# Delta heads 2 and 3 pause for eight rounds behind their second step, and six more output pieces stand beside the last rounds

## What is computed

```python
o_a = sliding_window_attention(qa, ka, va, sinks)    # 8 query heads, window 128
o_b = gated_delta_rule(qb, kb, vb, g, beta)          # 4 heads of 128, chunks
o_b = o_b * rsqrt(mean(o_b * o_b) + eps) * norm_w * silu(z)
return concatenate([o_a, o_b], axis=-1) @ w_out      # 1024 x 1024
```

```python
v_new = u_c - w_c @ S
o_c = q_c @ S + qk_c @ v_new
S = S * exp(gl_c) + kt_c.T @ v_new
```

## Time and profile before

| what | value |
|---|---|
| median of 3 runs | 2363.33 us (2363.24 to 2363.87) |
| profiled execution | 2363.01 us |
| its span in the trace | 2360.9 us |
| PE busy | 2318.6 us, 98% |
| DVE, ACT, POOL busy | 1425.1, 1076.6, 262.5 us |
| mean granted TensorE clock | 0.998 |

### The profile page before, as it was taken

One profiled execution on the slowest core, in us unless ns is written; L12 is line 12 of the kernel. 1 busy time (PEld: TensorE's weight loads), 2 busy tenths in 40 slices (PEclk: granted clock), 3 DMA queues, 4 the chain that ended last, 5 costly groups with the idle time before them and its releaser, 6 DMA issues.

```text
span 2360.9 us, 32407 instructions
## 1 busy us (share of the span) xinstructions
PE 2318.6 (98%) x13256; PEld 1945.5 (82%) x13258; DVE 1425.1 (60%) x2184; ACT 1076.6 (46%) x1853; POOL 262.5 (11%) x235
## 2 busy tenths in 40 slices
PE   9998999999999999999999999999999999999997
PEld 7777888888888988888968888888887779888886
DVE  6786764434587753433775677636486446775455
ACT  5655363223278542322555654434254555444341
POOL 0041320000221400000420011100000001110000
PEclk9999999999999999999999999999999999999999
DMA  5220133233223233222221232232221112322222
GB/s 210 81 67 3 39 106 98 98 98 97 82 99 98 81 107 98 97 93 96 96 81 59 77 99 98 99 98 91 92 94 55 53 39 95 101 93 96 98 90 63
DMA packets 60643, 207.48 MB, mean 88 GB/s; under 512 B 7072, under 2 KB 9168, under 8 KB 60368
## 3 DMA queue, kind: packets, MB, share of 16 engines
q1 hardware_dynamic: 59856, 202.66, 26.3%
q0 software_dynamic: 640, 2.76, 0.3%
HBM read 201.93 MB, written 2.10 MB: 86 GB/s over the span
## 4 chain that ended last, share of the span: by engine, by line
PE 85%; DVE 9%; ACT 3%; issue 1%; POOL 0%; DMA 0%; SPq 0%; another core or an unknown queue 0%; DVEq 0%; ACTq 0%; POOLq 0%
PE ps L288 25%; PE ps L290 25%; PE ps L289 25%; DVE WL L261 1%; DVE TM L633 1%; DVE AR L858 1%; PE ps L2908 1%; PE ps L348 1%; PE ps L2937 1%; PE ps L2921 1%; PE ps L350 1%; PE ps L349 1%; PE ps L1841 1%; DVE X L636 1%; DVE XL L658 0%
## 5 line engine op out<-in xcount | busy, mean ns | idle before, releaser
L288 PE MATMUL ps<-XH,WH 128*128 128x512 f32 (+1 forms) x2120 | 794.7, 375 | 8.2 <-DVE WL L831 5.8
L290 PE MATMUL ps<-XH,WL 128*128 128x512 f32 (+1 forms) x2120 | 779.4, 368 | 0.0
L289 PE MATMUL ps<-XL,WH 128*128 128x512 f32 (+1 forms) x2120 | 779.1, 367 | 0.0
L261 DVE TENSOR_TENSOR WL<-RAW,WH 128x1024 fp32r<-128x1024 f32 (+1 forms) x378 | 462.6, 1228 | 176.8 <-ACT WH L249 176.0
L288 PEld LDWEIGHTS ps<-XH,WH 128*128 128x128 f32 x2120 | 400.6, 189 | 85.8 <-issue 8.6
L249 ACT ACTIVATE WH<-RAW 128x1024 fp32r<-128x1024 f32 (+1 forms) x378 | 386.8, 1035 | 153.5 <-DMA RAW<-in_w 124.2
L290 PEld LDWEIGHTS ps<-XH,WL 128*128 128x128 f32 x2120 | 400.4, 189 | 66.4
L289 PEld LDWEIGHTS ps<-XL,WH 128*128 128x128 f32 x2120 | 400.9, 189 | 65.4 <-issue 2.2
L288 PE MATMUL ps<-H,WH 128*128 128x512 f32 (+1 forms) x1200 | 431.0, 359 | 1.6 <-DVE AR L858 1.0
L289 PE MATMUL ps<-H,WH 128*128 128x512 f32 (+1 forms) x1200 | 429.5, 358 | 0.0
L290 PE MATMUL ps<-H,WL 128*128 128x512 f32 (+1 forms) x1200 | 429.5, 358 | 0.0
(11 more groups left out here) (426 smaller groups left out, 2337.3 us busy)
## 6 DMA issues: line engine op xcount, KB each, us to landing
RAW<-in_w SPq DMA_DIRECT2D x128, 512.0 KB, 3.4
RAW<-in_up SPq DMA_DIRECT2D x88, 512.0 KB, 3.4
RAW<-in_dn SPq DMA_DIRECT2D x32, 512.0 KB, 3.4
RAW<-in_hyb SPq DMA_DIRECT2D x20, 512.0 KB, 3.4
RAW<-in_qkv SPq DMA_DIRECT2D x18, 512.0 KB, 3.5
RAW<-in_kvf SPq DMA_DIRECT2D x17, 512.0 KB, 3.5
RAW<-in_rin SPq DMA_DIRECT2D x16, 512.0 KB, 3.4
RAW<-in_dn SPq DMA_DIRECT2D x16, 384.0 KB, 3.0
```

The costliest lines, as they stand in the source:

```text
L261: dve.e.tensor_tensor(WL[:, s, 0:n], RAW[:, s, 0:n], f32(WH[:, s, 0:n]), ALU.subtract).then_inc(*w_lo.at(u))
L288: pe.e.matmul(out, wh, xh, start=first, stop=False)
L289: pe.e.matmul(out, wh, xl, start=False, stop=False)
L290: return pe.e.matmul(out, wl, xh, start=False, stop=last)
```

## The change

`hybrid_rounds` leaves heads 2 and 3 out of rounds 3 to 10 (`rounds` counts the finished ones, so 2 to 9), on all four engines. When heads 0 and 1 are over, six more pieces are added to those that `ahead(2)` may use.

```diff
+        LATE = 8
+
         def hybrid_rounds(heads, att, ahead):
-            over, rounds, left = set(), 0, 12
+            over, rounds, left, more = set(), 0, 12, 6
             while len(over) < 5:
-                for g in heads[0:2] + [att] + heads[2:4]:
+                for g in heads[0:2] + [att] + (heads[2:4] if rounds < 2 or rounds >= 2 + LATE else []):
                     if g not in over and next(g, "end") == "end":
                         over.add(g)
                 rounds += 1
+                if heads[0] in over and heads[1] in over:
+                    left, more = left + more, 0
                 if att in over and left and rounds >= 28:
                     ahead(2)
                     left -= 2
-            ahead(left)
+            ahead(left + more)
```

## The result

The changed kernel takes 2376.97 us (median of 4 runs, 2373.03 to 2379.85) beside 2363.3 us before (2363.24 to 2363.87). The ratio on record is 1.0052, with a 95% interval of 1.004 to 1.0064: 12.3 us slower, 9.5 to 15.1 by the interval. The profiled execution took 2376.9 us. Two things are to be seen at once: the loss is twice the forecast, and the runs of the changed kernel lie 6.8 us apart, where those of the kernel before lay within 0.7 us.

The account below looks back on a forecast made before the run. TensorE bounds the kernel, carrying 85% of the chain. Terms: -4.0 won, +8.0 steps moved, -4.3 today's waits and handovers replaced, +1.4 at round 20 and w, +5.0 tail: +6.1, 2369.4 us; range 2365.8 to 2372.6.

Parts of the forecast that it names:

- The gain of rounds 3 to 10: Window rounds without heads 2 and 3: the window's loop of 3.4 us limits them, so round 20 begins 4.0 us earlier.
- No wait in this stage did that today: Clock rule: a 2.20 us wait elsewhere halved TensorE's clock, none in this stage; the new 2.5 us wait might.
- The steps of rounds 20 to 33: Heads 2 and 3 run eight steps late: 8.0 us of TensorE steps move behind the window; norms begin at 254.6.
- the walk: The prediction's round-by-round timing of the changed stage, from the window's maxima at 163.51 to the stage's end at 279.7.
- The wait at w: Round 23, w products: one wait of 1.15 us where three stand in a row today.
- The tail: From the norms' start to the stage's end: 25.1 us, with 2.5 us idle before the last six pieces.
- Rival (1): TensorE's clock falls behind the new wait before head 2's pieces: +7.7 us, 2371.0; chance 0.20.
- The six pieces themselves are moved, not added: nothing: The six pieces put beside the last rounds add no time of their own.
- Rival (2): A smaller loss: the woken heads' value blocks hide and w doesn't wait; +3.3 us, 2366.6; chance 0.20.
- (3): Not slower: the window's loop is no bound, rounds 3 to 10 fall to 2.8 us; -0.8 us, 2362.5; chance 0.08.
- (4): The six pieces find heads 0 and 1 unready and stand as waits: +8 us, 2371.3; chance 0.04.

Follow-up runs that it names:

- the repeat: Experiment 1: the changed kernel run again unaltered; 2374.51 us (2373.00 to 2378.75) beside 2364.06 before, ratio 1.0044.
- fill_all: Changed kernel with unread products of ones added in TensorE's waits of rounds 4, 5, 6, 8 and behind head 3's norm; 2374.15 us beside 2364.7.
- experiment 8: Changed kernel with heads in the order 0, 2, 1, 3 from round 21 on; 2375.67 us beside 2364.06 before, ratio 1.0048.
- experiment 6: Changed kernel without the six pieces beside the last rounds, 12 there and 12 behind; 2374.76 us beside 2365.2 before, ratio 1.0036.
- experiment 9: Changed kernel with heads 2 and 3 left out of two rounds instead of eight; 2372.62 us beside 2364.06 before, ratio 1.0032.

## Why the prediction was wrong, step by step

**The sign and the order of events were right, the size was half.** The likeliest time was 2369.4, +6.1; measured is +12.3 by the ratio, outside the range. Two steps of the prediction failed: the term for the steps moved behind the window was 2.3 us too small (29.9 us for 27.6), and the clock was priced at one wait only, as a rival, where the first trace lost 4.5 us at two.

- *The gain of rounds 3 to 10 (4.0 us)*: right where the clock stays or falls once. The repeat has it within 0.4 us at every step from 4 to 13, and the first w 3.8 us earlier. In the first profiled execution of the changed kernel it was 0.8.
- *"No wait in this stage did that today"* is where the clock went wrong: true of the kernel before, whose longest wait in the stage is 1.17 us, and not of the changed one. I priced the fall only at the new last wait. But the pause also makes a wait of 2 us in round 4 (1.96 in the profile for 1.09 before, near the 2.20 of rows 8), since TensorE loses heads 2 and 3's transposes there, and one of 1.8 us in round 8 for 0.85. I had counted 4 us of new waiting in the start without asking how long each piece of it is. The clock was low there for some 10 us in this execution (3.0 us lost, against the repeat), for some 3 in the repeat, and not in fill_all.
- *The steps of rounds 20 to 33* is the term of the sum that was mis-sized: 27.6 us from the first w to the norms in the walk (227.0 to 254.6), 29.9 in the traces with a pause of eight rounds and the heads in their old order. I added up products from rounds in which all four heads do steps of one shape. With heads 2 and 3 eight steps behind, each round goes from 128x128 to 64x64 and back, and experiment 8 prices that at 0.3 us. Experiment 1's rounds 24 to 30 carry just that, 2.3 us together.
- *The wait at w*: 1.15 in the walk, 0.87 measured; right.
- *The tail*: 25.1 us in the walk, 25.5 without a fall, 27.0 with it. The order of events (idle before pieces 13 and 14, behind VectorE's finals, 2.5 us before the last six) came as written. Rival (1) came in the first trace, at 1.5 us, and not in the repeat. It came on top of the forecast, not in its place.
- *"The six pieces themselves are moved, not added: nothing"*: right, as far as it can be measured: without them the loss is 9.6 us for the repeat's 10.5 (experiment 6).
- *Rival (2)*, a smaller loss, is out: the value blocks took their 5.6 us and w its wait. *(3)*, not slower, is out: no maxima follow each other by less than 3.2 us, and that only behind a narrow block; plain rounds keep 3.3 or more. *(4)* is out: TensorE idled 0.18 us before piece 13 and 0.39 behind VectorE's finals, where the walk had 0.3 and 0.7.

So structure alone is 6.4 (walk) + 2.3 (shapes) + 0.5 (rests) = 9.2, and the falls added 4.5 us more in the first trace. With 9.2 the time would be 2372.5, at the very edge of the range: the size of the mixed rounds took up all its room, and the falls carried the first trace out of it. The runs go on to 2379.85, and that part no trace shows. The range was too narrow on both counts: it had no row for a mixed round, and it took one fall for the most.

## What to carry to other kernels

Shifting one of two interleaved groups fills nothing if the other group's loop is a latency chain: here TensorE gave up 8 us of products beside the window and got back 4, and the 8 had to be paid later, next to steps of another shape. When a plan takes work off an engine, list the length of each wait that it leaves, not their sum: a wait of 2 us can cost the clock behind it, in some executions and not in others, and a kernel whose runs begin to spread is telling so. When a tail moves, ask what covered it: the pieces that stood behind the last round were the cover for the last head's normalization. Putting them back doesn't win the time by itself: in experiment 6 the last wait is gone, and 2.23 us of waiting stand in round 35 instead.

## What the runs showed of the hardware

**The clock.** TensorE's granted clock went to half (1.2 GHz) near waits of 1.8 to 2.6 us in this stage, mostly for 3.4 us, once for 10.2 (first trace, 161.2 to 171.4); 512-column products started 0.43 us apart for 0.23. The same waits don't always bring it: the wait of 1.96 us in round 4 is in the repeat as well, with a third of the low time, and the wait of 2.56 us before the last pieces had a fall in the first trace and none in the repeat. Products put into the waits took the falls away (1.00 throughout the stage in fill_all), and with them most of the spread (1.0 us for 5.8). The Trainium skill (TensorE: Matmul & The Clock Gate, "What's actually happening") says that activity releases a clock that is throttled otherwise; that agrees.

**Change of shape.** Going between products of 64x64 and 128x128 costs TensorE 0.3 us there and back, though nothing is waited for: four steps whose products come to 1.9 us take 2.16 us with one such change and 2.51 with two (experiment 8). The Trainium skill (TensorEngine Tiling (Array Packing), "Key Properties") says that a change of tiling mode, not just of tile, drains the engine. The rows of experiment 8 agree with that and give the price of a change, which I hadn't asked of a trace before the prediction.

**VectorE and GpSimd.** A cast that takes 0.43 us took 1.37, and a three-operand product 1.56 for 0.75, while GpSimd multiplied two tiles in memory (experiment 9). The Trainium skill (SBUF — State Buffer, "Who interferes with whom") says that VectorE has one pair of memory ports to itself and shares a second with GpSimd, and that the shared pair is locked by one instruction at a time; the trace fits that, but no run here took GpSimd's product away to show it.
